# Moving a layer's rate products, its last key tile, and the gate of its retention to other places in a two-block transformer kernel

## The reference

```python
y_a, v_first = rwkv7_mixer(p_a, ...)      # 4 heads of 64: a delta-rule recurrence
y_b = retention_mixer(p_b, positions)     # 4 heads of 64: decayed attention in chunks
y_c = mla_mixer(p_c, positions, ...)      # 8 heads: softmax attention, low-rank q, k and v
h = h + concatenate([y_a, y_b, y_c]) @ w_out[l]
h = h + (silu(gate) * up) @ w_down[l]
```

## Time and profile before

| what | value |
| --- | --- |
| three runs | 2068.2, 2073.46, 2074.24 us, median 2073.46 |
| the profiled execution | 2072.65 us, span 2070.9 us, mean granted TensorE clock 0.986 |
| PE busy (12552 matmuls) | 2001.1 us, 97% of the span |
| DVE busy | 1116.6 us, 54% |
| ACT busy | 827.1 us, 40% |
| POOL busy | 88.9 us, 4% |
| DMA queues | 22.8% of 16 engines' span |

### The profile page before, as it was taken

One profiled execution on the slowest core, in us unless ns is written; L12 is line 12 of the kernel. 1 busy time (PEld: TensorE's weight loads), 2 busy tenths in 40 slices (PEclk: granted clock), 3 DMA queues, 4 the chain that ended last, 5 costly groups with the idle time before them and its releaser, 6 DMA issues.

```text
span 2070.9 us, 29232 instructions
## 1 busy us (share of the span) xinstructions
PE 2001.1 (97%) x12552; PEld 1610.4 (78%) x12552; DVE 1116.6 (54%) x1553; ACT 827.1 (40%) x1165; POOL 88.9 (4%) x61
## 2 busy tenths in 40 slices
PE   7998899999999999988999999999999999899998
PEld 6785587888888887747788888887778777689887
DVE  7557756543344544567564434447757664343274
ACT  4246534322222323564342222235555554334273
POOL 4000120000000000103100000000000000010000
PEclk9999899999999999998999999999999999999999
DMA  6220011222322322100132232224222222212202
GB/s 229 97 74 11 2 44 62 102 89 84 122 101 71 109 87 84 62 1 3 43 104 100 77 117 102 89 83 144 84 100 74 92 79 102 102 51 93 72 3 91
DMA packets 26336, 167.35 MB, mean 81 GB/s; under 512 B 2912, under 2 KB 3168, under 8 KB 10464
## 3 DMA queue, kind: packets, MB, share of 16 engines
q1 hardware_dynamic: 26208, 165.48, 22.8%
HBM read 163.38 MB, written 2.10 MB: 80 GB/s over the span
## 4 chain that ended last, share of the span: by engine, by line
PE 89%; DVE 7%; ACT 2%; issue 1%; DMA 1%; SPq 0%; DVEq 0%; ACTq 0%
PE bank L675 25%; PE bank L677 25%; PE bank L676 25%; PE bank L701 5%; PE bank L907 3%; DVE ring_low L1986 1%; PE bank L808 1%; DVE bank L2232 1%; ACT ring_high L1448 1%; PE bank L921 1%; DVE arena L2245 1%; PE bank L1313 1%; PE bank L1332 1%; DMA ring<-slabs_in 1%; DVE arena L2296 0%
## 5 line engine op out<-in xcount | busy, mean ns | idle before, releaser
L675 PE MATMUL bank<-arena_split,ring_high 128*128 128x512 f32 x2188 | 866.0, 396 | 22.4 <-DVE ring_low L2088 10.0
L676 PE MATMUL bank<-arena_split,ring_high 128*128 128x512 f32 x2188 | 854.5, 391 | 0.0
L677 PE MATMUL bank<-arena_split,ring_low 128*128 128x512 f32 x2188 | 854.3, 390 | 0.0
L675 PEld LDWEIGHTS bank<-arena_split,ring_high 128*128 128x128 f32 x2188 | 412.6, 189 | 119.8 <-issue 14.7
L676 PEld LDWEIGHTS bank<-arena_split,ring_high 128*128 128x128 f32 x2188 | 412.6, 189 | 89.0 <-issue 4.8
L677 PEld LDWEIGHTS bank<-arena_split,ring_low 128*128 128x128 f32 x2188 | 412.4, 188 | 86.9
L1986 DVE TENSOR_TENSOR ring_low<-ring,ring_high 128x2048 fp32r<-128x2048 f32 (+3 forms) x160 | 341.1, 2132 | 196.5 <-ACT ring_high L1448 196.0
L1448 ACT ACTIVATE ring_high<-ring 128x2048 fp32r<-128x2048 f32 (+3 forms) x160 | 283.0, 1769 | 388.6 <-PE bank L677 386.7
L1466 ACT ACTIVATE arena<-bank 128x512 f32<-128x512 f32 x72 | 43.1, 598 | 285.5 <-DVE bank L1967 285.4
L1967 DVE TENSOR_TENSOR bank<-bank,rstd 128x512 f32<-128x512 f32 x72 | 50.2, 698 | 116.3 <-PE bank L677 116.3
L1416 ACT ACTIVATE arena<-bank 128x512 f32<-128x512 f32 (+1 forms) x77 | 44.4, 594 | 139.9 <-PE bank L677 62.6
(11 more groups left out here) (345 smaller groups left out, 1815.7 us busy)
## 6 DMA issues: line engine op xcount, KB each, us to landing
ring<-slabs_in SPq DMA_DIRECT2D x121, 1024.0 KB, 4.8
ring<-slabs_in SPq DMA_DIRECT2D x32, 704.0 KB, 4.0
ring<-slabs_in SPq DMA_DIRECT2D x5, 512.0 KB, 3.7
con<-con_in SPq DMA_DIRECT2D x1, 2208.0 KB, 9.5
h<-x_in SPq DMA_DIRECT2D x4, 512.0 KB, 7.2
out<-arena SPq DMA_DIRECT2D x8, 256.0 KB, 2.1
ring<-slabs_in SPq DMA_DIRECT2D x2, 768.0 KB, 4.2
arena<-gates_in SPq DMA_DIRECT2D x1, 1536.0 KB, 9.3
```

Source lines behind the costliest of these rows:

```text
L675: pe.matmul(out, weight[0], right[0], start=start, stop=False)
L676: pe.matmul(out, weight[0], right[1], start=False, stop=False)
L677: return pe.matmul(out, weight[1], right[0], start=False, stop=stop)
```

## The change

The line numbers of the changed kernel are higher by up to 9 from the `mla` part on. What moves, in both layers:

- TensorE: the four products `z` go ahead of the key tiles. The fourth key tile leaves its place ahead of the values and goes into step 3 of the score loop. `attended` of the last pair of heads goes ahead of the second half of the retention scores.
- ACT: the sigmoids of `z` and the table load go ahead of the key copies, the fourth key's copy ahead of the exponentials of unit 3.
- DVE: all masks of the second half come ahead of `keys`. The gate of the retention (one multiplication for each half) moves into the first level of the inverse, ahead of each output multiplication.
- POOL: `k_carried` waits for `inverse_ready` too.
- Arena tiles: two latent tiles go to other places (`LAT_LOW`), the transposed inverse from 23 to 31, and `U` from 31 to 23.

```diff
-        LAT_HIGH, LAT_LOW = [47, 48, 49, 50, 51], list(range(25, 30))
+        LAT_HIGH, LAT_LOW = [47, 48, 49, 50, 51], [25, 26, 27, 28, 52]
...
                     gemm(("qrot", l, g), "dve", rows, [cst("rot_mla")], [A(43 + g)[:, 0, :]])
-                for m in range(MLA_H // 2):
+                decay_and_rate(l)
+
+                def key_tile(m):
+
                     split_gemm(("kn", l, m), "act", split_tiles(split_slab(f"kv_up{l}"), m * KVT * P, KVT), kv_lat,
                                parts_step if m == 0 else None)
+
+                for m in range(MLA_H // 2 - 1):
+                    key_tile(m)
                 for j in range(NT):
...
-                decay_and_rate(l)
                 pe.wait_ge(krope_spread, cnt.next(krope_spread))
...
                 for u in range(len(units) + 3):
+                    if u == 3:
+                        key_tile(MLA_H // 2 - 1)
                     if u < len(units):
...
+                attended(MLA_H // 2 - 1)
                 retention_scores(l, 1)
-                attended(MLA_H // 2 - 1)
...
-                        blocks(("T1", l, n, e), "act", 19 + e, 23 + e)
+                        blocks(("T1", l, n, e), "act", 19 + e, 31 + e)
...
-                for m in range(MLA_H // 2):
-                    both_heads(("kn", l, m), 31 + 2 * m)
-                for j in range(NT):
-                    copy_out(("vt", l, j), A(39 + j)[:, 0, :])
-
                 act.wait_ge(krope_spread, cnt.next(krope_spread))
                 for n, (dst, bias) in enumerate(((25, "w0"), (29, "a0"))):
...
                 act.preload_act_table_set(ROOTS)
+                for m in range(MLA_H // 2 - 1):
+                    both_heads(("kn", l, m), 31 + 2 * m)
+                for j in range(NT):
+                    copy_out(("vt", l, j), A(39 + j)[:, 0, :])
+
                 act.wait_ge(praw_used, cnt.next(praw_used, 3))
                 for u in range(MLA_H * NT + 4):
                     w = u - 4
+                    if u == 3:
+                        both_heads(("kn", l, MLA_H // 2 - 1), 29 + MLA_H)
...
-                        if hp == 1 and j == 1:
-                            keys()
                     if hp == 0:
                         removal_key()
+                keys()
                 decayed()
-                for hp in range(2):
-                    dve.wait_ge(*taken(("ry", l, hp)))
-                    tt(A(39 + hp)[:, 0, :], A(39 + hp)[:, 0, :], A(23 + hp)[:, 0, :], MUL).then_inc(cnt.up(dve_done), 1)
-                dve.wait_ge(cnt.sem, cnt.value)
...
                 def retention_output(hp):
 
+                    dve.wait_ge(*taken(("ry", l, hp)))
+                    tt(A(39 + hp)[:, 0, :], A(39 + hp)[:, 0, :], A(23 + hp)[:, 0, :], MUL).then_inc(cnt.up(dve_done), 1)
                     dve.wait_ge(*taken(("rss", l, hp)))
+                    dve.wait_ge(cnt.sem, cnt.value)
                     tt(A(2 + hp)[:, 0, :], A(39 + hp)[:, 0, :], A(hp)[:, 0, :], MUL).then_inc(cnt.up(mix_ret_ready if hp else dve_done), 1)
...
-                Xt, X = A(23, 2), A(21, 2)
+                Xt, X = A(31, 2), A(21, 2)
...
                         pool.wait_ge(k_decayed, l + 1)
+                        pool.wait_ge(inverse_ready, 2 * (l + 1))
                         pool.tensor_tensor(chunked(27), chunked(12), end, ALU.mult).then_inc(cnt.up(k_carried), 1)
```

12 lines of the change are left out of this document (6 added, 6 removed).

## The result

| | before | after |
|---|---|---|
| median | 2068.2 us (7 runs, 2062.49 to 2074.24) | 2055.64 us (7 runs, 2053.03 to 2061.2) |
| profiled execution, span | 2072.65, 2070.9 us | 2055.64, 2053.9 us |
| mean granted clock | 0.986 | 0.990 |

The ratio is 0.9939, 95% interval [0.9926, 0.9953]: 12.6 us faster (9.7 to 15.3). The forecast was 7.7 us and 2065.0, with a range down to 2059.0. In the later rounds its medians were 2070.38, 2069.97 and 2069.54 (24, 17 and 18 runs), so 2068.2 is the lowest of four medians. For the same reason the two traces lie further apart (17.0 us of span) than the medians: the execution of before that was profiled is one of its longer ones, that of after has just the median.

The account below looks back on a forecast made before the run. PE, busy 97%, was taken to bound the kernel, so time comes only from its waits and half-clock stretches. Score start 6.4, steps 2 to 4 0.8, clock 0.5: 7.7 us off 2072.65 gives 2065.0, range 2059.0 to 2070.5.

Parts of the forecast that it names:

- step 5: Inverse's first level: its low clock costs 2.7 us per layer; bounds -2 to +2.7, taken as +0.25 each, 0.5 us gained.
- Step 1: Start of the score loop: rates made ahead of the keys, fourth key tile covering the first exponential; 6.4 us, both layers.
- Step 2: `attended` ahead of the second retention scores delays DVE's masks: 0.95 us lost in layer 0, 3.5 in layer 1.
- Step 3: All masks ahead of the delta keys changes DVE's overlap with POOL: 0.8 us lost in layer 0, 1.85 gained in layer 1.
- Step 4: Gate and `k_carried` off the way to the inverse: 3.3 us less 1.2 given back, net 2.1 us gained per layer.
- the third rival: First level of the inverse at full clock in both layers: 12.6 us gained, 2060.0 us; chance 0.20.
- my list: Three places per layer where PE waits or runs at half clock: score-loop start, delta keys on DVE, inverse's first level.

Follow-up runs that it names:

- scores_alone: Kernel before with only the rates ahead of the keys and the fourth key tile in the score loop; 2062.31 us against 2070.38, ratio 0.9962.
- rates_alone: Kernel before with `z`, its sigmoids and the table load ahead of the keys, all four key tiles in their old place; 2062.96 us, ratio 0.9964.
- attended_back: Changed kernel with the last `attended` behind the second retention scores again; 2052.06 us, ratio 0.9917 to the kernel before.
- delta_alone: Kernel before with all of the change except the moved rates and key tile (`attended`, masks, gate, POOL's wait, arena tiles); 2066.34 us, ratio 0.9982.
- no_pool_wait: Changed kernel with POOL's `k_carried` no longer waiting for the inverse; 2062.76 us, ratio 0.9961 to the kernel before.
- masks_back: Changed kernel with the delta keys inside the second half's masks again; 2054.31 us, ratio 0.9933 to the kernel before.
- k_later: Changed kernel with `attended` behind the second retention scores and POOL's decayed-key product waiting for DVE's last gram input; 2058.31 us, ratio 0.9948 to the kernel before.
- fill_grams: Changed kernel with three products of constants on PE ahead of the wait for the gram products' inputs; 2056.24 us, ratio 0.9934 to the kernel before.
- gate_back: Changed kernel with the two gate multiplications between `decayed` and the inverse again; 2063.22 us, ratio 0.9975 to the kernel before.
- fill_level: Kernel before with products of constants on PE in the wait ahead of the inverse's first level; 2063.88 us against 2069.54, ratio 0.9974.

## Why the prediction was wrong

**What put it outside the range.** The measured time lies 3.4 us below the range's lower end. The term of the sum that is furthest off is no step of the change but the base: 2072.65, where seven runs gave 2068.2, so 4.45 of the 9.4 us between 2065.0 and 2055.64. From 2068.2 the forecast would have been 2060.5 and the range 2054.6 to 2066.1, with the result inside. The three runs shown ahead reached down to 2068.2, and the range should have carried that. The other 4.9 us are gain that the steps didn't have, and there step 5 failed.

**Step 1** (forecast 6.4) was right in its mechanism: no wait ahead of the first turned tile, which came at 171.01 (forecast 171.6). Unit 4's came 3.7 us earlier, counted from the first rotary product (forecast 3.0 to 3.7). The half-clock stretch at 176 is gone. By time step 1 is worth 7.9 us (scores_alone), and 6.4 lies inside the interval. The gain hangs on the rates more than I expected before those runs (rates_alone: 7.5 us for 4.8 expected). The loop's falls of clock are the part that I had priced only at its start. In the nine kernels of the table that have step 1, "scores" takes 64.6 and 64.4 us on average, in the three that have neither part of it 68.6 and 70.3: 4.0 + 5.9 = 9.9 us. Length times clock is 61.4 against 63.5 in layer 0 and 62.9 against 64.9 in layer 1 (after, before): only about 4 us are waiting and work at equal clock, the rest, in these two executions, is that fewer stretches run at 0.50. That the edit causes those fewer falls is argued from the averages, since one and the same stream differs by 6.5 us from one execution to the next (below).

**Step 2** (forecast -0.95 and -3.5) was right in layer 0, and in layer 1 its price isn't one number. With `attended` undone DVE's wait ahead of the masks is 0 and 1.12 us (attended_back), with it 1.02 and 3.43: it costs 1.0 and 2.3. I had expected a wait of over 5 in layer 1, since I took `attended` near half clock there; after it ran at full, in about 2.3. In delta_alone and no_pool_wait it ran at half, and the wait was 6.72 and 6.71: the wait that I forecast exists, in two of the six traces with this edit. Undoing it gives 4.5 us by the ratios but only 1.6 by the two delta stretches of the traces. Executions of the slower kind may make up the difference; that isn't shown.

**Step 3** (forecast +1.85 in layer 1 and -0.8 in layer 0): both signs were right, with the pair at 3.44 (forecast about 3.5) and L2274 at 0.69 (forecast 0.7). In layer 1 the size was wrong: the operation ahead of L2274 was to gain 0.55, but took 1.80 in place of 1.13, since the keys begin (922.69) while POOL's second mixing product (921.84 to 924.21) still runs. That leaves 0.6 of the 1.85. In sum nothing (masks_back, where the clock of the delta stretch in layer 1 is also lower, 0.92 against 0.96). A DVE operation with both inputs in SBUF doesn't get through beside a POOL operation: the pair took 3.44 us beside it and 1.29 without it (k_later). The Trainium skill (SBUF — State Buffer, "SBUF: two separate sides") calls the shared port pair an exclusive lock; the two rows agree.

**Step 4** (forecast +2.1 a layer) was about right. From the gram products' start to the level's start layer 0 takes 7.90 us in place of 9.28, though the gram products take 1.54 longer; with these at 3.03 it takes 6.91 (fill_grams), 2.4 us less. Both edits are needed for the short wait: with either undone PE waits 2.3 to 4.5 us ahead of the level, and the time is 7.5 (gate_back) and 4.5 us longer (no_pool_wait).

**Step 5 is the step that failed.** It had both bounds (-2 to +2.7 a layer), took +0.25, and gave a level at full clock in both layers only 0.20. The level ran 2.2 and 2.4 us faster (4.6 together), against 1.5 and 0.6 lost in the gram products: 2.5 in place of 0.5. The condition of the third rival is what came about, but that its 12.6 us are also the 12.6 measured is luck. It had 6.4 for the scores and 5.4 for the level; measured were 7.9 for the scores, 3.7 for the delta part (scores_alone, delta_alone), and 2.5 net for the clock around the level. Its reason (no gap between slow gram products and the level) held in part, as PE still waits 1.42 and 0.32.

The reason that I had named against it ("layer 1's wait of 3.16 sufficed for a fall") didn't hold, as that wait isn't there any more: after the change PE waits only 1.42 and 0.32 ahead of the level, where it waited 4.36 and 3.16. I had worked out in step 4 that the chain ahead of the level gets shorter, but had not carried the shorter wait into step 5. With the waits written out, the fast level was the likelier case in layer 0; in layer 1 the unchanged code ran it fast as well in two other traces (scores_alone 6.08, rates_alone 6.09), so how much of its 2.4 us the change brings isn't shown. Fill_level then showed the price by itself: 5.4 us for two levels at full clock, with the waits left in place. The Trainium skill (TensorE: Matmul & The Clock Gate, "HAM oscillation — how this bites in real kernels") has it that work behind an idle gap starts cold; fill_level's rows agree, and so do the changed kernel's gram products behind their new wait of 2.63 (4.57 and 4.79 us); those of gate_back in layer 0, at 3.03 behind the same wait, don't.

In layer 1 there was more: before, the second retention scores ran slowly too (930.45, 4.64 us for 16 matmuls, where after shows 2.42 for 14 and 0.48 for 2). That fall isn't in my list at all. With the low-rank products ahead of them (2.53 against 1.98) it is 2.3 us of PE's work, of the 5.1 us by which layer 1's delta stretch is shorter.

**What stays open.** Why a fall of the clock happens in one execution and not in the next isn't settled. attended_back and k_later have the same instructions up to layer 0's first retention score, and the stretch takes 68.00 us at 0.90 in the one and 61.52 at 1.00 in the other (windows of PE):

```profile
153.28:221.28 68.00, 60.34 (x257) 0.90 0.03 11
```

```profile
153.03:214.55 61.52, 53.86 (x257) 1.00 0.03 12
```

So single traces mix the edit with the falls that they happened to have, and only the ratios over many runs price an edit. Whether the masks' move should be kept with `attended` undone isn't settled either (0.9917 against 0.9923).

## What to carry to other kernels

Where one engine is busy 97% of the time, look first for the waits after which its clock falls: a wait is to be priced with the work behind it at half clock, and when an edit shortens a wait, ask whether the fall goes too. Two edits on one chain ahead of such a wait can each look small and still belong together: here either alone left a wait of 2.3 to 4.5 us, behind which the level was slow in one layer of two. A forecast's base is a term like the others: take it from the median of many runs, and put their spread into the range. An operation that is moved away from a neighbour with which it collides meets the next one; follow all readers of its result, too.

## What the runs showed of the hardware

- Three or four products of constants in a wait kept the granted clock up: 6.13 and 5.81 us for the level, 8.48 and 8.51 without them, and the level started no later.
- The same instruction stream ran at a mean clock of 1.00, 0.95 or 0.90 in different executions, 61.5 to 68.0 us for one stretch. Of the nine kernels with step 1, eight have a length of 61.5, 64.6 to 64.9 or 68.0 in layer 0, as if a fall cost about 3.3 us (an estimate from the distances of these lengths).
- Two DVE operations with both inputs in SBUF beside a POOL operation took 3.44, 3.08 and 3.06 us, and 1.3 without it, whatever the pair computes. Masks that read PSUM weren't held: the eight took 3.27 us with POOL idle (layer 0 after) and 3.27 with POOL busy from 919.41 on (layer 1).
